# Routing of a mixture layer: token rows turned inside the projection, scaled afterwards, order of experts first

## The reference

```python
x = x + g1 * y                                   # y: the mixer's output projection
h = rms_norm(x, norm_ffn[i]) * (1.0 + sc2) + sh2
logits = (t @ w_router).astype(jnp.float32)      # t = h, 512 x 1024
top_val, top_idx = lax.top_k(logits, TOP_K)      # 2 of 8
top_w = jax.nn.softmax(top_val, axis=-1)
for e in range(N_EXPERTS):
    y_e = swiglu_ffn(t, w_gate_up[e], w_down[e]) # 1024 -> 2 x 1408 -> 1024
    out = out + combine[:, e:e + 1] * y_e
```

## Time and profile before

| | |
|---|---|
| runs, median of 3 | 2783.12 us |
| profiled execution | 2788.35 us |
| its span | 2787.1 us |
| TensorE busy | 2652.8 us, 95% |
| VectorE, ScalarE, GpSimd busy | 59%, 44%, 7% |
| granted TensorE clock, mean | 0.984 |

### The profile page before, as it was taken

One profiled execution on the slowest core, in us unless ns is written; L12 is line 12 of the kernel. 1 busy time (PEld: TensorE's weight loads), 2 busy tenths in 40 slices (PEclk: granted clock), 3 DMA queues, 4 the chain that ended last, 5 costly groups with the idle time before them and its releaser, 6 DMA issues. The chain is left out here.

```text
span 2787.1 us, 34082 instructions
## 1 busy us (share of the span) xinstructions
PE 2652.8 (95%) x13585; PEld 2163.6 (78%) x13585; DVE 1640.4 (59%) x2692; ACT 1217.1 (44%) x2095; POOL 182.7 (7%) x264
## 2 busy tenths in 40 slices
PE   6999999999999898899999999999999999999998
PEld 5777788887888897577777776787788777788887
DVE  6786564554874684554688887423334577553444
ACT  3676422223554343344577774422233456332222
POOL 0000000000000730200000010020100001000001
PEclk8999999999999999899999999999999999999999
DMA  6233254442232210535699992222321115222322
GB/s 244 80 130 116 106 197 166 151 172 92 97 117 99 64 69 30 206 133 202 242 348 359 362 373 103 82 86 88 125 85 56 65 42 206 74 102 87 110 83 72
DMA packets 87062, 391.65 MB, mean 141 GB/s; under 512 B 21514, under 2 KB 25646, under 8 KB 51118
## 3 DMA queue, kind: packets, MB, share of 16 engines
q1 hardware_dynamic: 73680, 353.53, 35.0%
q10 hardware_dynamic: 10190, 25.87, 2.7%
q0 software_dynamic: 3024, 9.98, 1.0%
HBM read 369.55 MB, written 25.57 MB: 142 GB/s over the span
## 5 line engine op out<-in xcount | busy, mean ns | idle before, releaser
L344 DVE TENSOR_TENSOR wlo<-stage,whi 128x1024 fp32r<-128x1024 f32 (+3 forms) x481 | 512.9, 1105 | 317.1 <-ACT whi L356 315.3
L356 ACT ACTIVATE whi<-stage 128x1024 fp32r<-128x1024 f32 (+3 forms) x481 | 437.4, 956 | 209.7 <-PE ps L696 178.5
L696 PE MATMUL ps<-whi,mxhi 128*128 128x512 f32 (+1 forms) x528 | 201.9, 386 | 11.2 <-DVE wlo L344 9.4
L696 PE MATMUL ps<-bxhi,whi 128*128 128x512 f32 x480 | 199.1, 415 | 8.7 <-DVE y0lo L344 4.0
L696 PE MATMUL ps<-wlo,mxhi 128*128 128x512 f32 (+3 forms) x528 | 195.0, 374 | 0.0
L696 PE MATMUL ps<-bxhi,wlo 128*128 128x512 f32 x480 | 189.0, 394 | 0.0
L696 PE MATMUL ps<-bxlo,whi 128*128 128x512 f32 x480 | 188.6, 393 | 0.0
L344 DVE TENSOR_TENSOR wlo<-more,whi 128x1024 fp32r<-128x1024 f32 (+1 forms) x126 | 142.8, 1175 | 49.3 <-ACT whi L356 48.4
L696 PE MATMUL ps<-whi,mxlo 128*128 128x512 f32 (+1 forms) x432 | 161.8, 375 | 0.0
L352 DVE SCALAR_TENSOR_TENSOR part<-stage,small,part 128x256 f32<-128x256 f32 x252 | 137.9, 547 | 9.0
L696 PE MATMUL ps<-lxhi,whi 128*128 128x512 f32 x352 | 140.4, 399 | 1.6 <-DVE lxlo L352 1.6
(11 more groups left out here) (640 smaller groups left out, 5941.6 us busy)
## 6 DMA issues: line engine op xcount, KB each, us to landing
stage<-in_gu SPq DMA_DIRECT2D x92, 1024.0 KB, 5.7
more<-in_gu SPq DMA_DIRECT2D x40, 1024.0 KB, 6.8
stage<-in_ada SPq DMA_DIRECT2D x39, 1024.0 KB, 4.8
stage<-in_dn SPq DMA_DIRECT2D x19, 1024.0 KB, 6.9
stage<-in_dn SPq DMA_DIRECT2D x24, 768.0 KB, 4.3
stage<-in_gin SPq DMA_DIRECT2D x16, 1024.0 KB, 4.8
stage<-in_gt SPq DMA_DIRECT2D x16, 1024.0 KB, 4.9
more<-in_dn SPq DMA_DIRECT2D x13, 1024.0 KB
```

The costliest lines, as they stand in the source:

```text
L344: return e.do.tensor_tensor(out, x, y, op)
L356: return e.do.activation(out, x, f, **kw)
L696: return self.p.do.matmul(out, lhsT, rhs, start=start, stop=stop, skip_group_check=True)
```

## The change

- The token rows are made from x times gain only (`xg`, a ring of three blocks), without the token's factor. TensorE turns them inside the projection (`pe_turn_x`, seven of eight blocks at the steps in `turns`), ScalarE copies them into `xrows`. Once the factors are known, ScalarE scales each block of 128 tokens (128x1024) by its column, and GpSimd adds the shift, which `pe_shift` has spread over all partitions. The stores take two token blocks each instead of two column halves.
- 28 of the 32 score products are put into the projection, from k = 16 on; they share one bank.
- The squares' sums are taken straight in column form: four products of one column with `sq` and four with the last square; the factor is Ln and Exp of 128x4.
- The order of experts (`ids`) comes ahead of the first pick; picks 0 to 2 and their token numbers, and the three gathers of expert 0, stand ahead of the branch, as do the turn and the split of tile 0 and the split of the first weight load. The flag comes later.
- SyncE issues two weight loads ahead of the branch without waiting for rows, and the third when tile 1's rows have landed.
- Expert 0 takes tile 0 with the first and the second load before tiles 1 and 2.

```diff
         self.gdn_dve(L)
+        self.xrows, self.xg = self.at("xrows", [P, 4, 1024], 78), self.at("xg", [P, 3, 512], 90)
+        self.shift, self.rst = self.at("shift", [P, 1024], 96)[:, :], self.spare[:, 76:80]
+        self.last_square = L.tmp[1], self.A(("go", "q", 7))
...
-        self.lb = [self.take(("lb", c), at=4 + c) for c in range(4)]
+        self.lb = self.take("lb", at=4)
+        turns = {12: 0, 14: 1, 20: 2, 23: 3, 30: 4, 36: 5, 45: 6}
         for k, _ in enumerate(self.pe_gemm("go", "go", range(1, 4), L.X, lambda q: [V(("gy", "l", q))])):
+            if k in (4, 6):
+                self.pe_shift(k // 2 - 2)
+            if k in turns:
+                self.pe_turn_x(turns[k])
             if k == 24:
                 ps, vacant = self.take("count")
                 p.wait_ge(V("wrs"), *vacant)
                 self.mm(ps[:, 0:8], self.c("ones"), self.wrs)
                 self.mm(ps[:, P:2 * P], self.c("ones"), self.c("tri")).then_inc(*P_.up("count"))
-            elif k >= 32:
-                self.pe_scores((k - 32) // 4, k % 4)
+            if 16 <= k < 40 or k >= 44:
+                self.pe_scores((k - 16) // 4 if k < 40 else 6, k % 4)
+        self.pe_token_sums(self.sq, V(("go", "t", 6)), False)
         for c in range(4):
-            self.pe_scores(4, c)
+            self.pe_scores(7, c)
+        self.pe_token_sums(*self.last_square, True)
...
+        z = self.mm(ps[:, 8 * c:8 * c + 8], self.x[:, m, c * P:(c + 1) * P], self.wrg[:, 8 * m:8 * m + 8], m == c == 0, m == 7)
+        if m == 7 and c == 3:
+            z.then_inc(*self.P.up("lb"))
...
+        ps, _ = self.lb
+        self.p.wait_ge(mark)
+        for c in range(4):
+            z = self.mm(ps[:, 32 + c:33 + c], squares[:, c * P:(c + 1) * P], self.c("ones")[:, 0:1], False, last)
+        if last:
+            z.then_inc(*self.P.up("token sums"))
...
+        ps, vacant = self.take(("shift", half), at=6 + half)
+        self.p.wait_ge(*vacant, self.V(("mod", 1, 3)))
+        for m in range(4):
+            o = 24 + 4 * half + m
+            z = self.mm(ps[:, m * P:(m + 1) * P], self.mod[1][:, o:o + 1].broadcast_to([P, P]), self.c("ident"))
+        z.then_inc(*self.P.up(("shift", half)))
...
+        ps, vacant = self.take(("hr", m), at=5 + m % 3)
+        self.p.wait_ge(self.V(("xg", m)), *vacant)
+        for c in range(4):
+            z = self.tr(ps[:, c * P:(c + 1) * P], self.xg[:, m % 3, c * P:(c + 1) * P])
+        z.then_inc(*self.P.up(("hr", m)))
...
+            self.act_square("go", 2 * n, L.tmp[0:2], 1.0, V(("gy", "l", 7)))
+            if n > 1:
+                self.act_turned_x(2 * n - 2)
+                self.act_turned_x(2 * n - 1)
+            self.act_square("go", 2 * n + 1, L.tmp[0:2], 1.0)
+            if n == 0:
+                for half in range(2):
+                    use = ("shift", half)
+                    a.wait_ge(self.P(use))
+                    act(a, self.shift[:, 512 * half:512 * half + 512], self.bank(use)[:, :], ACT.Copy).then_inc(*A.up(use, free(use)))
+            elif n == 1:
+                self.act_turned_x(0)
+                self.act_turned_x(1)
+        self.act_turned_x(6)
+        a.wait_ge(self.P("token sums"))
+        act(a, self.rst, self.bank("lb")[:, 32:36], ACT.Ln, bias=self.c("e6"), scale=1.0 / 1024).then_inc(*A.up(free("lb")))
+        a.wait_ge(A.now())
+        act(a, self.rst, self.rst, ACT.Exp, scale=-0.5).then_inc(*A.up("rst"))
...
-                if m:
+                v.wait_ge(V.now(), *([P_(("hr", m - 3))] if m > 2 else []))
+                ts(v, self.xg[:, m % 3, :], self.x[:, m, :], self.gain(1, 3)[:, m:m + 1], None, MUL).then_inc(*V.up(("xg", m)))
+                if 0 < m < 7:
                     self.dve_sum("go", m - 1, L.tmp[0:2])
+                if m == 6:
+                    self.dve_sum("go", 6, L.tmp[0:2])
...
     def route_pe(self, L):
-        p, P_, A, V = self.p, self.P, self.A, self.V
+        p, P_, V = self.p, self.P, self.V
         p.wait_ge(*self.fence)
-        blocks = [slice(c * P, (c + 1) * P) for c in range(4)]
-        self.pe_total("xs4", self.sq, V(("go", "t", 6)), more=self.last_square)
-        for m in (5, 6, 7):
-            for c in range(4):
...
-        def turn(m):
-            ps, vacant = self.take(("hr", m))
-            p.wait_ge(A(("rn", m)), *vacant)
-            for s in blocks:
-                z = self.tr(ps[:, s], L.tmp[m][:, s])
-            z.then_inc(*P_.up(("hr", m)))
...
-        for m in range(5):
-            turn(m)
         ps, vacant = self.take("ranks")
-        p.wait_ge(V("taken"), *vacant)
+        p.wait_ge(*vacant)
+        self.pe_busy(ps, 3)
+        p.wait_ge(V("taken"))
         self.mm(ps[:, 0:32], self.c("tri"), L.f(6))
         self.mm(ps[:, 32:64], self.c("ones"), L.f(6)).then_inc(*P_.up("ranks"))
-        for m in range(5, 8):
-            turn(m)
-        self.pe_came(L, 0)
+        for n in range(3):
+            self.pe_came(L, n)
+        for q in (0, 4):
+            ps, vacant = self.take(("x", 0, 0, q))
+            p.wait_ge(*vacant)
+            self.pe_busy(ps, 0 if q else 6)
+            p.wait_ge(self.Dahead[0]("row"))
+            for m in range(q, q + 4):
+                z = self.tr(ps[:, (m - q) * P:(m - q + 1) * P], L.rows[0][:, m * P:(m + 1) * P])
+            z.then_inc(*P_.up(("x", 0, 0, q)))
...
-        self.pe_busy(ps, (2, 3, 0, 0)[n])
...
     def route_act(self, L):
         a, A, P_, V = self.a, self.A, self.P, self.V
         a.wait_ge(*self.fence)
-        self.pin("natural_log_exp_and_others")
-        self.act_rstd("xs4", 1024, "e6", L.rs, "rs4")
+        self.act_turned_x(7)
+        for c in range(4):
+            a.wait_ge(A.now())
+            act(a, self.xrows[:, c, :], self.xrows[:, c, :], ACT.Copy, scale=self.rst[:, c:c + 1]).then_inc(*A.up(("scaled", c)))
+        self.act_ahead("gu1_0", 0, False)
+        for q in (0, 4):
+            use = ("x", 0, 0, q)
+            a.wait_ge(P_(use))
+            act(a, L.X[0][:, q:q + 4, 0:P], self.bank(use)[:, :].rearrange("p (m n) -> p m n", m=4), ACT.Copy).then_inc(*A.up(("xh", 0, 0, q)))
...
+        then(tt(v, w64, inner(rk), outer(self.c("io8")), EQ))
+        then(tt(v, w64, w64, inner(self.c("io8")), MUL))
+        then(v.do.tensor_reduce(s8[:, 3, :], w64, AX, ADD))
+        then(v.do.tensor_copy(L.ids, s8[:, 3, :]), "ids")
...
         pick(0)
+        pick(1)
+        self.dve_came(L, 0)
+        pick(2)
+        self.dve_came(L, 1)
         then(tt(v, w64, outer(rk), inner(self.c("io8")), EQ))
         then(tt(v, w64, w64, inner(self.c("lim")), MUL))
         then(v.do.tensor_reduce(key, w64, AX, ADD))
         then(tt(v, key, run, key, GT))
         then(v.do.tensor_reduce(m3[:, 0:1], key, AX, MAX))
         then(v.do.tensor_copy(L.flag, m3[:, 0:1]), "flag")
-        self.dve_came(L, 0)
-        then(tt(v, w64, inner(rk), outer(self.c("io8")), EQ))
-        then(tt(v, w64, w64, inner(self.c("io8")), MUL))
-        then(v.do.tensor_reduce(s8[:, 3, :], w64, AX, ADD))
-        then(v.do.tensor_copy(L.ids, s8[:, 3, :]), "ids")
         then(tt(v, m3, m2, m1, SUB), "gap")
-        for n in range(1, 4):
-            pick(n)
+        self.dve_came(L, 2)
+        self.dve_ahead("gu1_0", 0, False)
+        for q in (0, 4):
+            use = ("x", 0, 0, q)
+            v.wait_ge(A(("xh", 0, 0, q)))
+            h = L.X[0][:, q:q + 4, 0:P].bitcast(F32)
+            tt(v, L.X[1][:, q:q + 4, 0:P], self.bank(use)[:, :].rearrange("p (m n) -> p m n", m=4), h, SUB).then_inc(*V.up(("xl", 0, 0, q), free(use)))
+        pick(3)
...
     def route_pool(self, L):
-        g, V = self.g, self.V
+        g = self.g
         g.wait_ge(*self.fence)
+        for c in range(4):
+            g.wait_ge(self.A(("scaled", c)))
+            tt(g, self.xrows[:, c, :], self.xrows[:, c, :], self.shift, ADD).then_inc(*self.G.up(("row", c)))
         g.wait_ge(*[self.Dh[c]("hrows") for c in range(2)])
-        self.pool_came(L, 0)
+        for t in range(3):
+            self.pool_came(L, t)
 
     def pool_came(self, L, t):
...
     def route_sync(self, L):
         s = self.s
-        for half in range(2):
-            cols = slice(512 * half, 512 * half + 512)
-            s.wait_ge(self.A(("hrow", 4 * half + 3)))
-            s.do.dma_start(self.d["hrows"].rearrange("(c p) f -> p c f", p=P)[:, :, cols], L.rows4[:, :, cols]).then_inc(*self.Dh[half].up("hrows", by=16))
+
+        def rows(half):
+            two = slice(2 * half, 2 * half + 2)
+            s.wait_ge(self.G(("row", 2 * half + 1)))
+            s.do.dma_start(self.d["hrows"].rearrange("(c p) f -> p c f", p=P)[:, two, :], self.xrows[:, two, :]).then_inc(*self.Dh[half].up("hrows", by=16))
+
+        rows(0)
+        rows(1)
         s.wait_ge(self.V("ids"))
         load = lambda r: self.nc.values_load(L.ids[0:1, r:r + 1], engines=[mybir.EngineType.SP], min_val=0, max_val=7)
         self.expert = [load(0)]
-        self.sync_load(self.place["gu1_0", 0] + 1)
```

(26 more changed lines are left out.)

99 lines of the change are left out of this document (35 added, 64 removed).

## The result

| | before | after |
|---|---|---|
| median | 2782.78 us (6 runs, 2781.93 to 2785.01) | 2797.36 us (6 runs, 2794.43 to 2805.77) |
| profiled execution | 2788.35 us | 2798.5 us |
| its span, granted clock | 2787.1 us, 0.984 | 2797.2 us, 0.984 |
| TensorE busy | 2652.8 us | 2654.0 us |

The ratio is 1.0055, with a 95% interval of 1.0042 to 1.0069: slower by 0.5%, 14.6 us, and outside the predicted range. The sign was the one I had forecast, the size was not.

What follows compares the result with a forecast made beforehand. TensorE, busy 95% of the span, was taken to bound the kernel. Projection +8.1, gather -0.3 and the stretch behind it -1.9 gave +5.9: 2794.3 us profiled, 2789.0 as a median; stated range 2779 to 2796.

Steps and rivals of the forecast that it cites:

- The sign: Whole kernel: the change makes it slower, +5.9 us.
- step 6: From the gather to the end of the second weight load: 1.9 us won, bounds 6 won to 3 lost.
- Step 1: Layer-2 output projection: extra score products, transposes and shift products on TensorE add 8.1 us, bounds 6 to 12.
- the term for the scores: In the projection: twelve more score products at 0.23 us each add 2.8 us.
- Steps 2 and 3: Routing: token factor ready at E+3.6, selection 5.8 us sooner; VectorE's undisturbed chain done at E+17.3 against E+24.9.
- Step 4: Token rows: four GpSimd additions at 2.15 us end at E+14.0; the gather would be free at E+18.4.
- Step 5: Selection: GpSimd additions hold VectorE's two-SBUF-input operations; gather at E+25.5, its 7.4 us advantage reduced to 0.3.
- The small operations: Rival, selection: VectorE's short operations slip between GpSimd's additions; gather at E+18.4, sum -1.2, 2782 us; chance 0.20.
- Slower by more: Rival, projection and lock: 0.6 us bank waits per turn and longer additions, +11 to +12, 2795 us; chance 0.12.
- The damped case: Rival, stretch to 1700 us: near the transfer limit, shifts either way are damped, 2786 us; chance 0.08.

Runs made afterwards that it cites:

- late scores: Changed kernel with the twelve extra score products moved from the projection to behind it; 2800.34 us, ratio 1.0063 to the kernel before.
- no filler: Changed kernel without the six filler products ahead of the turn of tile 0; 2791.57 us, ratio 1.0026 to the kernel before.
- zero fills: Changed kernel with each GpSimd addition of the shift replaced by three zero fills of a scratch tile; 2791.01 us (one run).
- no additions: Changed kernel without GpSimd's four additions of the shift, stores waiting for ScalarE; 2792.68 us, ratio 1.0029 to the kernel before.
- quarters: Changed kernel with each GpSimd addition of 1024 columns cut into four of 256; 2798.64 us, ratio 1.0050 to the kernel before.
- rows by VectorE: Changed kernel without fillers, VectorE scaling the token rows and adding the shift instead of ScalarE and GpSimd; 2786.68 us, ratio 1.0017 to the kernel before.

## Why the prediction was wrong

The forecast was +5.9, the medians gave +14.6. By the stretches (means of two looks each) the difference of 8.7 is 4.5 in step 6 (-1.9 forecast, +2.6 measured), 2.3 at the gather (-0.3 and +2.0) and 2.3 behind the end of the second load, where the prediction put nothing, less 0.3 in the projection.

**Step 1, the projection, +8.1: right.** +7.8, without a gap for a bank. The late scores confirm the term for the scores.

**Steps 2 and 3, factor and chain: right.** The factor is ready at E+3.5 (forecast E+3.6), and without the lock the ranks stand at E+8.6 (by step 3's terms E+9.1).

**Step 4, the additions: right.** 2.31 a piece, forecast 2.15; the last ends at E+14.8, forecast E+14.0.

**Step 5, the lock: right in its mechanism, 1 to 2 us short at the gather.** The product of the chosen experts starts at E+16.0, forecast E+15.9 (in the second look at E+16.7). That it agrees to 0.1 is in part luck: the additions ended 0.8 later than forecast, and five small operations were left behind them, not eight. From there to the gather I allowed 9.6 and it took 10.8. Of this 0.7 is my own arithmetic: the row before shows 1.05 from the copy of the token numbers to the gather, and I wrote 0.3. The rest is the way from the pick to the token numbers (2.7, and not 2.3), which in the changed kernel lies in a stretch at half clock and has the second pick in it.

**Step 6, from the gather to the end of the second load: this step failed.** I forecast the gather + 32.2 (a gain of 1.9) and it was +36.0 and +36.4. Its terms, in the first look:

| | forecast | measured |
|---|---|---|
| gather to the turn | 6.6 | 8.85 |
| turn to the first product | 5.4 | 2.1 |
| first product to the second load's first | 4.9 | 7.5 |
| from there to the turn of tile 1 | 2.7 | 4.45 |
| from there to the end of the second load | 12.6 | 13.1 |

The first two nearly cancel. I took the landing of before, 6.6, for that of after; it was 4.4. In all three executions of the kernel before it is 6.6 to 7.2, in all nine with the changed rows 4.3 to 4.6. Which of the differences does it is not shown: the stores have another form, and the first weight load is issued 0.9 behind the gather before (1143.18) and 5.3 ahead of it after (1142.90). And I let the turn start at landing, though the code puts twelve filler records between, twice as many as in before, where I had myself noted that they ran over by 2.1. They ran 4.4 over. In return TensorE's branch did not show at all; only without the fillers do the 4.3 that I had charged appear, as 4.54. That queued products cover the branch is my reading of these two rows. The last three lines are the loss. Counted from the turn, the second load's first product came at 9.6, where I had 10.3: the branches together were not the mistake. Because the tile was turned late, ScalarE and VectorE came late to them, and the products behind them ran at a lower clock. ScalarE in time, then VectorE:

```profile
1157.69 1.08 ACT L356 ACTIVATE mxhi<-ps 128x512 fp32r<-128x512 f32 x2 [7.77 <-PE ps L699]
...
1158.89 1.28 ACT L776 ACT_TABLE_LOAD   x1
1161.95 2.00 ACT L356 ACTIVATE whi<-stage 128x1024 fp32r<-128x1024 f32 x2 [1.78 <-issue]
```

```profile
1158.32 1.29 DVE L344 TENSOR_TENSOR mxlo<-ps,mxhi 128x512 fp32r<-128x512 f32 x2 [5.33 <-ACT mxhi L356]
...
1165.34 2.38 DVE L344 TENSOR_TENSOR wlo<-stage,whi 128x1024 fp32r<-128x1024 f32 x2 [3.69 <-issue]
```

VectorE's split of the second load comes 7.0 after that of the tile; 3.69 of it is its branch (`issue`: it waits for nothing that the profile shows). TensorE stands still for 4.49, and its clock falls. Busy time by stretch, the changed kernel and the one without fillers (length; TensorE, weight loads, VectorE, ScalarE, GpSimd; clock, DMA share, GB/s):

```profile
1137.00:1148.00 11.00, 3.89 (x18) 3.75 (x18) 7.82 (x35) 0.09 (x1) 0.00 (x0) 0.50 0.61 227
1148.00:1157.00 9.00, 9.00 (x24) 5.28 (x25) 3.94 (x12) 1.92 (x2) 3.79 (x3) 0.70 0.81 266
1157.00:1166.00 9.00, 4.06 (x21) 2.97 (x19) 3.75 (x11) 4.46 (x6) 3.78 (x4) 1.00 0.45 146
1166.00:1171.00 5.00, 4.38 (x12) 3.47 (x13) 1.72 (x2) 0.00 (x0) 3.78 (x5) 0.66 1.02 413
```

```profile
1153.60:1164.00 10.40, 5.79 (x17) 4.65 (x18) 4.79 (x13) 4.58 (x6) 4.21 (x6) 0.50 0.61 199
1164.00:1181.00 17.00, 15.35 (x75) 11.73 (x75) 6.27 (x10) 4.69 (x9) 6.51 (x7) 0.99 0.70 256
```

The fillers bring the clock from 0.50 to 1.00, but it is spent on 9 us in which TensorE is idle more than half the time, and has fallen to 0.66 when the second load's products run. Without fillers the clock is 0.50 for the first load and 0.99 from then on. Twelve products at 0.23 would be 2.8: 1.7 of the table's fourth line is the clock.

**The rest, +2.4 behind layer 3's start: not settled.** The prediction put nothing here, since TensorE is dense from the second load on and a shift should pass one for one. The stretch took 1054.7 in both looks of before, and 1054.9 to 1057.5 in the eight edited kernels, whose work there is the same, in no order that follows the edits. It goes with the clock in the 50 us from 70 us behind `rtmp`: where that is 0.93 (both looks of after, no filler, zero fills) the stretch takes 1057.1 to 1057.5, where it is 0.97 (both looks of before, no additions, quarters, late scores) 1054.7 to 1055.3, and at 1.00 (the other three) 1055.8 to 1057.0. The step from 0.97 to 0.93 over 50 us is worth 2.0, an estimate from these two values. What decides between them no run here shows, so that the 2.4 may be a matter of the execution and not of the change.

**The rivals.** The small operations did not slip. "Slower by more" came nearest in size (2795), for another reason: no turn waited before E. The damped case fell: the stretch behind the second load took 552.9 to 554.4 in all twelve executions, while its start lay anywhere from 1167 to 1187, so as far as layer 3 a shift passes one for one. "3 lost if the waits for the second load and half clock add up" stood in step 6 as a bound, and 2.6 were lost. With +7.8, +2.0 and +2.6 the sum would have been 12.4, or 2795.5 as a median, just inside the stated range; the measured time lies 1.9 above that, near the 2.4 of layer 3.

## What to carry over

Give GpSimd no instruction that reads SBUF while VectorE runs a chain of short operations with two SBUF inputs: each of them lasts as long as GpSimd's instruction, however small it is. Zero fills, which only write, leave these alone but hold some operations with one input. When a change moves a wait, count again the filler work in front of it against the new length of the wait, and follow the late start through every engine that stands behind it, branches included. A gain at one landmark is worth only what arrives at the next point from which the bounding engine runs dense: here 9 us at the gather were 4 to 5 there without the additions, where VectorE's branch took 2.5 longer, and 7 to 8 were 7 to 8 with the zero fills.

## What the runs showed of the hardware

- A 128x32 operation of VectorE with two SBUF inputs takes 0.19 us alone, up to 0.70 beside GpSimd additions of 256 columns, 2.0 to 2.3 beside those of 1024, and 0.19 beside zero fills of 1024 (1.02 each). A TENSOR_SCALAR of 128x8, one input, takes 0.17 alone and up to 0.73 (128x4) beside the zero fills.
- TensorE's branch costs 4.54 us when nothing is queued and does not show with twelve filler records queued. VectorE's branch cost 3.7 to 3.9 in three executions and 6.3 in three others; ScalarE stood 1.6 and 1.8 in the two looks of the changed kernel and 4.7 and 4.9 in the two with rows by VectorE.
- The gather of tile 0's 128 rows lands 4.3 to 4.6 us after it starts in the nine executions with the changed rows, 6.6 to 7.2 in the three of the kernel before.
- The kernel before, timed against itself, differed by 0.1%.
